# Joint attention, last 16 jobs: the value products of a job's two heads alternate between two column halves, and the turned tiles get four slots

## The reference

```python
def gqa_attention(q, k, v):
    bsz, nq = q.shape[0], q.shape[1]
    q = q.reshape(bsz, nq, B_KV_HEADS, B_REP, HEAD_DIM)
    s = jnp.einsum('bqgrd,bkgd->bgrqk', q, k) * (HEAD_DIM ** -0.5)
    p = jax.nn.softmax(s.astype(jnp.float32), axis=-1).astype(v.dtype)
    o = jnp.einsum('bgrqk,bkgd->bqgrd', p, v)
    return o.reshape(bsz, nq, B_WIDTH)
```

## Time and profile before

| | |
|---|---|
| median of 3 runs | 2754.79 us (2754.7 to 2754.88) |
| the profiled execution, its time | 2751.06 us |
| its span, first to last instruction | 2749.2 us |
| PE busy, share of the span | 96% |
| mean TensorE clock granted | 0.98 of full |
| DMA in the attention stage | about nothing (0 to 2 GB/s) |
| attention stage, first scores to the end of the last product | 1545.4 to 1728.0 us |
| of these, rounds `j` = 18 to 33, of which the change speaks | 1622.4 to 1728.0 us |

### The profile page before, as it was taken

The page is one execution under the profiler, slowest core; times in us unless marked ns, Lnnn a source line. Parts: engine busy times, 40 slices in busy tenths (PEclk is TensorE's granted clock), DMA queues, the critical chain, the costliest instruction groups (busy, mean ns, idle before and its releaser), DMA issues.

```text
span 2749.2 us, 38078 instructions
## 1 busy us (share of the span) xinstructions
PE 2635.6 (96%) x13182; PEld 2186.7 (80%) x13182; DVE 1604.5 (58%) x2532; ACT 1052.5 (38%) x1666; POOL 263.9 (10%) x201
## 2 busy tenths in 40 slices
PE   7999899999999999999989998889999899899997
PEld 6886688887889988888778776678888787788886
DVE  6753665656667756565665774455555665644445
ACT  5334422223347752222343365452233422533333
POOL 2320100001121010000031000210000300300002
PEclk9999999999989999999999999999999999999999
DMA  3221344444310024444431000224444243232222
GB/s 129 68 92 62 112 148 145 145 145 130 122 47 1 2 95 143 145 145 145 145 108 62 31 1 1 69 75 147 145 145 138 84 142 118 85 107 99 99 92 77
DMA packets 77707, 274.33 MB, mean 100 GB/s; under 512 B 8353, under 2 KB 11809, under 8 KB 77089
## 3 DMA queue, kind: packets, MB, share of 16 engines
q1 hardware_dynamic: 58560, 205.55, 22.0%
q10 hardware_dynamic: 19040, 67.36, 7.3%
HBM read 270.78 MB, written 2.10 MB: 99 GB/s over the span
## 4 chain that ended last, share of the span: by engine, by line
PE 83%; DVE 7%; ACT 5%; issue 3%; DMA 1%; POOL 0%; ACTq 0%; DVEq 0%; SPq 0%
PE banks L2265 60%; PE banks L2402 5%; PE banks L2308 3%; PE banks L2696 3%; PE banks L2804 2%; DVE w_lo L1327 2%; PE banks L2783 2%; PE banks L2664 1%; ACT w_hi L672 1%; PE banks L2679 1%; PE banks L2763 1%; PE banks L2436 1%; DMA w_raw<-weights 1%; PE banks L2611 1%; DVE attn_nm L2138 1%
## 5 line engine op out<-in xcount | busy, mean ns | idle before, releaser
L2265 PE MATMUL banks<-h_hi,w_hi 128*128 128x512 f32 x1600 | 630.1, 394 | 3.9 <-DVE w_lo L1327 3.3
L2265 PE MATMUL banks<-h_hi,w_lo 128*128 128x512 f32 x1600 | 624.0, 390 | 0.0
L2265 PE MATMUL banks<-h_lo,w_hi 128*128 128x512 f32 x1600 | 623.9, 390 | 0.0
L672 ACT ACTIVATE w_hi<-w_raw 128x1024 fp32r<-128x1024 f32 x367 | 385.7, 1051 | 540.9 <-PE banks L2265 428.6
L1327 DVE TENSOR_TENSOR w_lo<-w_raw,w_hi 128x1024 fp32r<-128x1024 f32 x367 | 483.9, 1319 | 158.7 <-ACT w_hi L672 138.9
L2265 PE MATMUL banks<-g_hi,w_hi 128*128 128x512 f32 (+1 forms) x1108 | 429.6, 388 | 18.3 <-DVE w_lo L1327 14.3
L2265 PE MATMUL banks<-g_lo,w_hi 128*128 128x512 f32 (+1 forms) x1108 | 423.9, 383 | 0.0
L2265 PE MATMUL banks<-g_hi,w_lo 128*128 128x512 f32 (+1 forms) x1108 | 423.9, 383 | 0.0
L2265 PEld LDWEIGHTS banks<-h_hi,w_hi 128*128 128x128 f32 x1600 | 301.1, 188 | 72.3 <-DVE w_lo L1327 7.9
L2265 PEld LDWEIGHTS banks<-h_lo,w_hi 128*128 128x128 f32 x1600 | 301.3, 188 | 63.1 <-issue 1.7
L2265 PEld LDWEIGHTS banks<-h_hi,w_lo 128*128 128x128 f32 x1600 | 301.1, 188 | 63.2
(11 more groups left out here) (399 smaller groups left out, 3507.8 us busy)
## 6 DMA issues: line engine op xcount, KB each, us to landing
w_raw<-weights SPq DMA_DIRECT2D x384, 512.0 KB, 3.2
ada_raw<-ada ACTq DMA_DIRECT2D x112, 512.0 KB, 3.3
x<-x SPq DMA_DIRECT2D x4, 512.0 KB, 6.8
out<-x SPq DMA_DIRECT2D x8, 256.0 KB, 2.2
mix_cum<-ret_tab ACTq DMA_DIRECT2D x1, 1024.0 KB, 4.8
rows_c<-c_rows ACTq DMA_DIRECT2D x1, 1024.0 KB, 5.4
nsa_w<-cmp_w ACTq DMA_DIRECT2D x1, 1024.0 KB, 7.1
nsa_cbias<-nsa_cbias ACTq DMA_DIRECT2D x1, 1024.0 KB, 9.5
```

The costliest lines, as they stand in the source:

```text
L672: act.activation(w_hi[s][:], w_raw[s][:], ACT.Copy).then_inc(w_hi_done, 1)
L2265: mm = pe.matmul(bank, w[s][:, k, :], m[:, k, :], start=(n == 0 and a == 0), stop=(n == kts - 1 and a == 2))
```

## The change

Product: from `t` = 16 on, both lots of a job are multiplied in one go (`add_two_lots`), and their chunks alternate: chunk 0 of the first head in columns 0 to 63, chunk 0 of the second in columns 64 to 127, chunk 1 of the first, and so on. The number of matmuls is the same, 12 for each job, 24 instructions.

Order on PE in round `j` of part B: scores of `j`, turn of the first lot of job `j`-2, both products of job `j`-3, turn of the second lot of job `j`-2.

Slots: the lots of part B use `attn_pt` and the two slots of `attn_comb`, which part A no longer needs by then: four in all (`probs`). The copy of `t` waits for the product of `t`-4, and that of 18 and 19 for none.

Order on ACT: the copy of the first lot now stands ahead of both exponentials. The copy of an output tile of part B stands one lot later (`O_READY_AT`).

```diff
-O_READY_AT = {(4 * (u + 1) if u < 4 else 16 + 8 * (u - 3)): (u, ...
+O_READY_AT = {(4 * (u + 1) if u < 4 else 17 + 8 * (u - 3)): (u, ...
...
+        def probs(t):
+            return B4["comb" if t >= 16 and t % 4 > 1 else "pt"][:, t % 2, :]
...
             def copy_lot(t):
                 act.wait_ge(a_t, t + 1)
-                if t > 1:
+                if 1 < t < 18:
                     act.wait_ge(a_o, t - 1)
-                act.activation(B4["pt"][:, t % 2, :], turned, ACT.Copy).then_inc(a_tk, 1)
+                if t >= 20:
+                    act.wait_ge(a_o, t - 3)
+                act.activation(probs(t), turned, ACT.Copy).then_inc(a_tk, 1)
...
+                if len(lots) > 1:
+                    copy_lot(lots[0])
+                    lots = lots[1:]
                 if j < ATT_JOBS:
...
                     exponentials(j, 0)
-                    if len(lots) > 1:
-                        copy_lot(lots[0])
-                        lots = lots[1:]
                     exponentials(j, 1)
...
+            def add_two_lots(t):
+                u = out_tile(t)
+                pe.wait_ge(a_tk, t + 2)
+                if t in (16, 24):
+                    pe.wait_ge(a_hi, u - 1)
+                if t in (32, 40):
+                    pe.wait_ge(g_ready, G_BEFORE["attn_in"] + u - 5)
+                m, qi = (t - 16) // 8, (t - 16) // 2 % 4
+                values = B2["bv"][:, :, 64 * (m // 2):64 * (m // 2) + 64]
+                for k in range(KEY_TILES):
+                    for half in range(2):
+                        o = psum[u % 2][64 * half:64 * half + 64, qi * P:(qi + 1) * P]
+                        mm = pe.matmul(o, values[:, k, :], probs(t + half)[:, k * P:(k + 1) * P], start=(k == 0),
+                                       stop=(k == KEY_TILES - 1))
+                        if k == KEY_TILES - 1:
+                            mm.then_inc(a_o, 1)
...
-                    for t in TURNS[j - 2]:
-                        turn_lot(j - 2, t)
-                        if t:
-                            add_lot(t - 1)
-            add_lot(N_TURNS - 1)
+                    first = TURNS[j - 2][0]
+                    turn_lot(j - 2, first)
+                    if 0 < first < 17:
+                        add_lot(first - 1)
+                    elif first:
+                        add_two_lots(first - 2)
+                    if first > 15:
+                        turn_lot(j - 2, first + 1)
+            add_two_lots(N_TURNS - 2)
```

More of the change, by code:

```diff
@@ L160, in out_tile @@
     return t // 4 if t < 16 else 4 + (t - 16) // 8
-O_READY_AT = {(4 * (u + 1) if u < 4 else 16 + 8 * (u - 3)): (u, (4 * (u + 1) if u < 4 else 16 + 8 * (u - 3)) - 1)
+O_READY_AT = {(4 * (u + 1) if u < 4 else 17 + 8 * (u - 3)): (u, (4 * (u + 1) if u < 4 else 16 + 8 * (u - 3)) - 1)
               for u in range(7)}
@@ L2768, in add_lot @@
                 pe.wait_ge(a_tk, t + 1)
[L2769 to L2781, removed]
+                if t in (8, 12):
+                    pe.wait_ge(a_hi, u - 1)
+                qi, h = t % 4, t // 4
+                o = psum[u % 2][:, qi * P:(qi + 1) * P]
+                values = B2["av"][:, :, h * P:(h + 1) * P]
                 for k in range(KEY_TILES):
-                    mm = pe.matmul(o, values[:, k, :], B4["pt"][:, t % 2, k * P:(k + 1) * P], start=(k == 0),
+                    mm = pe.matmul(o, values[:, k, :], probs(t)[:, k * P:(k + 1) * P], start=(k == 0),
                                    stop=(k == KEY_TILES - 1))
                 mm.then_inc(a_o, 1)
+            def add_two_lots(t):
+                u = out_tile(t)
+                pe.wait_ge(a_tk, t + 2)
+                if t in (16, 24):
+                    pe.wait_ge(a_hi, u - 1)
+                if t in (32, 40):
[9 more added lines that the diff above has]
+                            mm.then_inc(a_o, 1)
             for j in range(ATT_JOBS + 2):
```

## The result

| | before | after |
|---|---|---|
| first comparison: median of 4 runs each | 2754.74 us (2753.26 to 2754.88) | 2725.95 us (2721.7 to 2728.74) |
| ratio, with its 95% interval | | 0.9895 (0.9878 to 0.9913) |
| span of the profiled execution | 2749.2 us | 2724.4 us |
| first turn of round 18 to the copy of the last output tile | 103.53 us | 80.48 us |

The kernel became 28.8 us faster, 1.05%; a gain of 22.9 was forecast, in a range of times that went down to 2728.5 us. The stage itself took 23.05 us less. So the stage did what was worked out for it, and the other 5.7 us are not in it.

What follows compares the result with a forecast made beforehand. A chain of scores, maximum, exponential, copy, turn and product, not PE alone, bounds the 6.80 us round. Rounds 19 to 30 gain 21.60 us, the rest 1.4: 2754.79 - 22.9 = 2731.9 us, range 2728.5 to 2738.0.

Steps and rivals of the forecast that it cites:

- The pair costs one product: Part B, both products of a job together: 1.47 us, bounds 1.46 and, for two in turn, 2.92.
- run side by side: Products of lots 46 and 47 at the end: 7 matmuls alive in 0.20 us, against 4 with lot 46 alone.
- PE's row: PE from a round's first turn T: 0.80 + 1.47 + 0.80, next scores T + 3.07, next first turn T + 4.57.
- ACT's row: From first turn T through copy and both exponentials: head 1's scores at T + 3.53, then 1.50, a round of 5.03 us.
- Round 18, no gain: First round of the stage: 6.18 us after the change, 6.14 before.
- The tail: Stage after round 30, to the output copy's start: 14.04 us against 15.43, gain 1.4.
- The maximum and the output copies cost nothing: Part B: DVE's 3.04 us fit in 5.03; output copies (0.50 on ACT, three times) fall where ACT waits for a turn.
- Rival 1: Clock falls in the tail or another stretch behind it: 3 to 4 us, 2735 to 2737; chance 0.25, mostly upward.
- Rivals 2, 3 and 4: Column halves take turns, 2749.4, 0.04; PE sets the round, 2726.4, 0.05; denser rounds at 1.2 GHz, 2781, 0.03.
- the gain counts against any of them: Gain of 22.9 us applies to the median 2754.79 (giving 2731.9), the profiled execution or its span (2726.3) alike.
- a half-clock stretch that moves out: Just behind the stage (1741.5 to 1755 us): a stretch costing 3.0 us could vanish, 2728.9; range's lower end 2728.5.

Runs made afterwards that it cites:

- by threes: The changed kernel with the chunks of the two heads alternating in groups of three (6 instructions of a head): 2721.83 us in a single run, rounds of 5.02 us.

## Why the prediction was right in the stage and wrong in the total

Point by point:

- *The pair costs one product* (1.47): right. 0.80 to T + 2.26, 24 instructions in 1.53 us. But the ground given, that column halves "run side by side", lacked its condition. By the single starts in that trace, nine of lot 46's twelve instructions had started (the ninth at 1726.44) when lot 47's first did (1726.48), so three stood ahead of it, not some four: just as many as the limit lets pass. The copy had released lot 47 at that very moment (1726.43), so the overlap could not show that there is a limit. That the changed kernel alternates, and so never meets it, is luck as far as this reasoning goes: without the alternation the pair costs 2.39.
- *PE's row* (next scores at T + 3.07) and *ACT's row* (T + 3.53, a round of 5.03): right, 3.07, 3.54 and 5.02. That ACT and not PE sets the round is shown from both sides: lengthening ACT's row gave 5.35, shortening it 4.87, and 0.26 us more of PE's own (by threes) changed nothing.
- *Round 18, no gain* (6.18): right, 6.15.
- *The tail* (14.04): right, 14.05.
- *The maximum and the output copies cost nothing*: right; in the waits above no ACT instruction waits for DVE.
- *Rival 1*, the clock in the tail: not in the three profiles of the changed kernel. PE was busy there for 10.90 of 14.05 us, six turns of 0.80 us among them, and kept 1.00. By the rule of the Trainium skill that rival 1 cites, on transposes and the clock, it would have fallen; these traces don't agree. In the profile of one other kernel whose tail is as thin (7.01 of 8.74 us) it fell to a mean of 0.81. What decides between the two is not shown.
- *Rivals 2, 3 and 4*: none came.

**The step that failed** is the base of the last subtraction, "2754.79 - 22.9": "the gain counts against any of them". Three runs within 0.2 us of each other looked like a firm base. Over 51 runs the same kernel has a median of 2751.5, and its times reach from 2742.9 to 2755.3; the three lay 3.3 us above the median, and the first comparison's four 3.2. The four of the changed kernel lay 2.1 us below its own median, 2728.05. 3.2 + 2.1 + 23.5 is the measured 28.8. With 2751.5 the sum would have given 2728.6, against 2728.05 over 15 runs. With the step went the lower end of the range: it lay 3.4 us under the forecast, for "a half-clock stretch that moves out", as a thing of one stretch behind the stage, though the prediction itself put what a measurement can tell at 5.5 us. The traces show such stretches all over the kernel, some of them in one execution and not in another; the span before the stage alone varied from 1623.72 to 1628.11 us over the three profiles of the changed kernel, with nothing changed in it. The profile that was at hand said so: it took 2751.06 us, 3.7 less than the median. That was noted and not used.

How much of the 28.8 belonged to which runs' clocks can't be told, since for the first runs of the kernel before they are not listed. Of 47 later runs of the kernel before, 9 were as slow as the fastest of those four (2753.26) or slower. That all four were is far more than these counts would suggest. Why stays open.

**Where the 23 us came from.** From 6.80 a round: the copy's place on ACT gives 6.02 (-0.78); pair, alternation and slots together give 5.02 (-1.00 more). With one part left out of the changed kernel: without the slots 6.54, without the alternation 5.49, without overlap 6.15, with the copy in its old place 5.35. The parts don't add (leaving out the slots costs 21.8 us of the stage, leaving out the overlap 19.5): each takes away a bound that hides another.

## What to carry to other kernels

When an engine waits in the middle of its list, look at what the releasing engine did before: here a copy stood behind two steps that needed newer data, and moving it was worth 0.78 us a round without any change to the matmuls. Work for disjoint parts of the array should alternate every few instructions (here up to four cost nothing to speak of, twelve cost 0.92 us a pair); being neighbours is not enough. And a gain worked out from a trace is to be compared with a median over many runs: a few runs that agree to 0.01% can still be 0.1% off.

## What the runs showed of the hardware

- Products in two column halves run at full pace beside each other, in the same PSUM bank: 24 instructions in 1.53 us, 12 in 1.52.
- TensorE started an instruction for another part of the array ahead of at most three that had not started, in every arrangement tried here: against one product's 1.46 us, the pair took 0.93 us more with 12 instructions of a head in a row, 0.27 with 6, 0.05 with 4, 0.01 with 2. The Trainium skill ("TensorE: Matmul & The Clock Gate", Part 3, The mechanism) says that matmuls keep program order in start and end, strictly; in these traces the starts don't across column halves: in order, 24 instructions at 0.11 us apart would take 2.6 us and more, and the pair of the run with the chunks in order took 2.39. In no run here did the second head end before the first, so whether one semaphore on the last instruction could vouch for both is not shown; each head has its own count in this kernel.
- The same kernel's time varies by 12 us (2742.9 to 2755.3) over 51 runs; the mean clock of the 47 for which it is listed lies between 0.979 and 0.984.
